# Where a two-way expert stage is joined: the joined norm moved into both ways, and identity products on TensorE around the join

## The reference

```python
def first_block(x, ...):
    for l in range(DEPTH):                                  # DEPTH = 2
        x = x + token_mixers(rmsnorm(x, mix_norm_g[l]), ...)
        h = rmsnorm(x, ffn_norm_g[l])
        if l % 2 == 0:
            x = x + swiglu(h, ffn_w1[l // 2], ffn_w3[l // 2], ffn_w2[l // 2])
        else:
            x = x + moe_ffn(h, router_w[l // 2], moe_w1[l // 2], moe_w3[l // 2], moe_w2[l // 2])
    return rmsnorm(x, final_norm_g)

def second_block(x, c, positions, ...):
    for l in range(DEPTH):
        mod = silu(c) @ ada_w[l] + ada_b[l]                 # shift_m, scale_m, gate_m, shift_f, ...
        h = rms_norm(x, g_pre_mix[l]) * (1.0 + scale_m) + shift_m
        q, k, v, u = split(h @ w_in[l] + b_in[l])
        ...
```

## Time and profile before

| | us |
|---|---|
| median of three runs | 2087.17 |
| lowest and highest of them | 2086.82, 2090.17 |
| the profiled execution | 2089.91 |
| its span, first to last instruction | 2088.1 |
| PE busy in it | 2020.0 |
| mean granted clock of TensorE | 0.988 |

### The profile page before, as it was taken

One profiled execution on the slowest core, in us unless ns is written; L12 is line 12 of the kernel. 1 busy time (PEld: TensorE's weight loads), 2 busy tenths in 40 slices (PEclk: granted clock), 3 DMA queues, 4 the chain that ended last, 5 costly groups with the idle time before them and its releaser, 6 DMA issues.

```text
span 2088.1 us, 24564 instructions
## 1 busy us (share of the span) xinstructions
PE 2020.0 (97%) x10120; PEld 1675.5 (80%) x10120; DVE 1627.6 (78%) x1556; ACT 1187.9 (57%) x1264; POOL 72.8 (3%) x97
## 2 busy tenths in 40 slices
PE   7999999999999999999999999999979999899998
PEld 6888788878887778888888888888767787787887
DVE  5777889756878779888988888888976986676454
ACT  6444454446454367777777777777735444444443
POOL 0000010000000000000000000001010000100000
PEclk9999999999999989999999999999989999999999
DMA  8443479854444458999999999999953898434551
GB/s 307 156 162 139 144 282 386 333 212 179 162 143 155 150 229 331 378 367 379 360 376 370 355 378 377 386 374 385 397 206 132 339 372 302 184 137 173 190 182 61
DMA packets 80321, 554.77 MB, mean 266 GB/s; under 512 B 9286, under 2 KB 11206, under 8 KB 14534
## 3 DMA queue, kind: packets, MB, share of 16 engines
q1 hardware_dynamic: 74160, 536.45, 67.9%
q10 hardware_dynamic: 5468, 14.60, 1.9%
q0 software_dynamic: 576, 2.10, 0.3%
HBM read 548.30 MB, written 4.82 MB: 265 GB/s over the span
## 4 chain that ended last, share of the span: by engine, by line
PE 86%; DVE 8%; ACT 3%; POOL 1%; issue 1%; DMA 1%; ACTq 0%; POOLq 0%; DVEq 0%
PE bank L455 81%; PE bank L482 2%; DVE wlo L1135 2%; ACT whi L1128 1%; POOL small L2363 1%; DVE xn L1715 1%; DMA raw<-in_moe_up 1%; DVE scoresB L1727 1%; DVE gate_tanh L1711 0%; DMA cols<-in_cols 0%; DVE x L2112 0%; DVE xn L2122 0%; PE bank L575 0%; PE bank L960 0%; DVE hTlo L1639 0%
## 5 line engine op out<-in xcount | busy, mean ns | idle before, releaser
L1135 DVE TENSOR_TENSOR wlo<-raw,whi 128x2048 fp32r<-128x2048 f32 x459 | 1045.5, 2285 | 268.1 <-ACT whi L1128 265.2
L1128 ACT ACTIVATE whi<-raw 128x2048 fp32r<-128x2048 f32 x459 | 876.2, 1913 | 355.5 <-PE bank L455 286.5
L455 PE MATMUL bank<-whi,hThi 128*128 128x512 f32 (+1 forms) x1088 | 430.0, 395 | 17.0 <-DVE hTlo L1639 7.4
L455 PE MATMUL bank<-whi,hTlo 128*128 128x512 f32 (+1 forms) x1088 | 421.7, 388 | 0.0
L455 PE MATMUL bank<-wlo,hThi 128*128 128x512 f32 (+1 forms) x1088 | 421.7, 388 | 0.0
L455 PE MATMUL bank<-whi,slots_hi 128*128 128x512 f32 x704 | 275.1, 391 | 2.4 <-DVE wlo L1135 2.3
L455 PE MATMUL bank<-whi,slots_lo 128*128 128x512 f32 x704 | 274.3, 390 | 0.0
L455 PE MATMUL bank<-wlo,slots_hi 128*128 128x512 f32 x704 | 274.2, 389 | 0.0
L455 PEld LDWEIGHTS bank<-whi,hThi 128*128 128x128 f32 x1088 | 208.0, 191 | 69.6 <-issue 14.0
L455 PEld LDWEIGHTS bank<-whi,hTlo 128*128 128x128 f32 x1088 | 208.1, 191 | 41.7
L455 PEld LDWEIGHTS bank<-wlo,hThi 128*128 128x128 f32 x1088 | 208.2, 191 | 39.5 <-issue 1.0
(11 more groups left out here) (332 smaller groups left out, 2269.8 us busy)
## 6 DMA issues: line engine op xcount, KB each, us to landing
raw<-in_moe_up SPq DMA_DIRECT2D x176, 1024.0 KB, 7.1
raw<-in_moe_down SPq DMA_DIRECT2D x88, 1024.0 KB, 7.0
raw<-in_w_in SPq DMA_DIRECT2D x72, 1024.0 KB, 4.8
raw<-in_ada_w SPq DMA_DIRECT2D x48, 1024.0 KB, 6.9
raw<-in_second_up SPq DMA_DIRECT2D x44, 1024.0 KB, 4.9
raw<-in_ffn_up SPq DMA_DIRECT2D x22, 1024.0 KB, 5.3
raw<-in_second_down SPq DMA_DIRECT2D x22, 1024.0 KB, 5.0
raw<-in_w_out SPq DMA_DIRECT2D x16, 1024.0 KB, 5.2
```

The lines of the kernel that those rows point to most:

```text
L455: m = mm(dst, l_, r_, start=start and i == 0, stop=stop and i == len(pairs) - 1)
L1128: s.then_inc(s.unit.activation(split_slots(p)[0][:, 0:n], slot_of_ring(raw, p, NRAW)[:, 0:n], ACT.Copy), ("hi", p), sem="weights_hi")
L1135: e.then_inc(e.unit.tensor_tensor(lo[:, 0:n], slot_of_ring(raw, p, NRAW)[:, 0:n], hi[:, 0:n].bitcast(F32), ALU.subtract), ("lo", p), sem=sem)
```

## The change

The joined norm of ACT and DVE is emitted inside each way, behind the engine's `_way_end` and behind the waits of `ways_joined`, which move there too; the jump over the other way comes after it. PE's waits stay behind its jump. In the joined norm both engines now split piece `q2` 0 ahead, before the features of tile 1. `normed(0)` stays behind the jump. PE gets `keep_clock`: 13 products of the identity with itself at the end of the sparse way, before PE raises its `_way_end`, and six behind the join; they write 128 columns of bank 7, which nobody reads. The dense way gets the six alone.

```diff
+            def keep_clock(n):
+                t.wait_ge(("free", t.held[7]) if 7 in t.held else None)
+                for i in range(n):
+                    m = mm(banks[7][:, 0:P], ident, ident, start=True, stop=True)
+                t.then_inc(m)
...
                 for step in behind_chunks:
                     run(step)
+                keep_clock(13)
...
                     two_ways(t, lambda: sparse_experts(l), lambda: dense_experts(l))
+                    keep_clock(6)
                     t.ahead = AHEAD
...
-        def two_ways(e, sparse, dense):
+        def two_ways(e, sparse, dense, behind=None):
...
                 e.own()
                 board.part = ""
                 e.unit.sem_inc(board.sem(e.done + "_way_end"), 1)
+                if behind is not None:
+                    e.passed, e.last = dict(start["passed"]), None
+                    ways_joined(e)
+                    behind()
                 return e.pieces, [e.counts.get(z) for z in ("weights_hi", "weights_lo")]
...
-            e.passed, e.last = dict(start["passed"]), None
+            if behind is None:
+                e.passed, e.last = dict(start["passed"]), None
+                ways_joined(e)
             if isinstance(e, Tensor):
                 e.held = {}
-            ways_joined(e)
...
+            def joined():
+                square_sum(x3[:, 1], 1, 1, ("squares", "final", 1))
+                features((0, "mix2"), None, (0,))
+                s.wait_ge(("gained", 1))
+                s.own()
+                square_sum(xn3[:, 1], 1, 3, ("squares", "modulated", 0, 0, 1))
+                load_attention(0)
+                s.split_ahead(("q2", 0, 0), 1)
+                features((0, "mix2"), None, (1,))
...
-                    two_ways(s, lambda: sparse_experts(l), lambda: dense_experts(l))
-            square_sum(x3[:, 1], 1, 1, ("squares", "final", 1))
-            features((0, "mix2"), None, (0,))
-            s.wait_ge(("gained", 1))
-            s.own()
-            square_sum(xn3[:, 1], 1, 3, ("squares", "modulated", 0, 0, 1))
-            load_attention(0)
-            features((0, "mix2"), None, (1,))
+                    two_ways(s, lambda: sparse_experts(l), lambda: dense_experts(l), joined)
             load_gate(0, 0)
...
                     v.then_inc(tensor(scaled[:, tt], xn3[:, tt], m3[:, 1, :], ALU.mult))
                     shift(tt)
+                v.split_ahead(("q2", 0, 0), 1)
                 features((0, "mix2"), None, (1,))
-                normed(0)
...
-                    two_ways(v, lambda: sparse_experts(l), lambda: dense_experts(l))
-            joined()
+                    two_ways(v, lambda: sparse_experts(l), lambda: dense_experts(l), joined)
+            normed(0)
```

## The result

The changed kernel takes 2090.81 us (median of 19 runs, 2087.54 to 2099.05) against 2086.24 for the kernel before (19 runs beside them): a ratio of 1.0023, 95% interval 1.0015 to 1.0031. That is 4.6 us slower. The forecast was 1.1 us slower (2088.2 against 2087.17); the time lies inside the range, 0.4 us from its upper end (2091.2), and the forecast has the right sign but a quarter of the size.

The account below looks back on a forecast made before the run. PE was taken as the bound, busy 2020.0 of 2088.1 us, losing most at the join. The terms moved the turn of the keys from 1547.23 to 1548.3, +1.1 us on 2087.17: 2088.2, range 2084.5 to 2091.2.

Parts of the forecast that it names:

- PE, the products: Around PE's jump at the join: thirteen products take 3.1 us, six take 2.6; the first turn comes 1.3 late.
- The clock: In PE's jump at the join, 3.95 us of standing: the clock falls, so the six products run at 1.2 GHz.
- From the first turn to the second: On PE behind the join: the turns of tile 1 come at 1538.0, 0.8 us behind the 1537.23 of before.
- DVE's piece split ahead: On DVE behind tile 1's shift: the 2.25 us piece is hidden just so by PE's work.
- The jumps themselves: Behind tile 1's features: ACT's jump 2.6 us, DVE's 2.9; ACT is the later, 1545.2 against 1544.75.
- 1.83 for `normed(0)`, bias and copies: On DVE behind its 2.9 us jump: this work takes 1.83 us, so DVE is through at 1544.75.
- The second fall of the clock: While PE stands 2.1 us ahead of the keys: a fall adds up to 2.4 us, in the range, not the sum.
- Rival (2): ACT's and DVE's moved jumps cost up to 2.6 us more under DMA load: +3.7, +6.1 with second fall; chance 0.17.
- Rival (1): The clock holds through PE's jump at the join, keys turn at 1545.95: -1.3 us, 2085.9; chance 0.17.
- Rival (3): PE's jump is short and the products work; tile 0's shift is the bound: about -3.8 us, 2083.4; chance 0.06.
- The measure: PE's turn of the keys, 1547.23 before: order and work behind it stay the same, so its shift is the end's.

Follow-up runs that it names:

- e3: The kernel before with the identity products alone (thirteen at the end of the sparse way, six behind PE's jump): ratio 1.0000 to the kernel before.
- e1: The changed kernel with eight one-column memsets ahead of DVE's first wait: ratio 1.0012 to the kernel before.
- e6: The same code as e1, run again: ratio 1.0013 to the kernel before.
- e9: The changed kernel with 128 one-column memsets ahead of DVE's first wait: ratio 1.0047 to the kernel before.
- e5: The kernel before with thirty one-column memsets ahead of DVE's first wait, so a border lies five instructions behind its landing: ratio 1.0018 to the kernel before.
- e4: The changed kernel with ACT's three loads moved from behind its jump into the first attention: ratio 1.0011 to the kernel before.
- e2: The changed kernel without the identity products, both the thirteen and the six: ratio 1.0028 to the kernel before.
- e11: e8 with one line changed, the attention's loads issued at the start of ACT's joined norm instead of right ahead of its jump: ratio 0.9997 to the kernel before.
- e12: e11 with the six identity products put back behind the join: 2085.53 us against 2089.52, ratio 0.9987 to the kernel before.
- e7: The changed kernel without identity products, with eight memsets ahead of DVE's first wait and ACT's three loads in the first attention: ratio 1.0020 to the kernel before.
- e8: The changed kernel with tile 1's features behind the jump, no products, no split ahead, sixteen memsets ahead of DVE's first wait: ratio 1.0006 to the kernel before.
- e10: e7 with no piece split ahead and sixteen memsets instead of eight: ratio 1.0004 to the kernel before.

## Why the prediction was right in sign and short in size

**PE, the products: right.** 3.06 us for thirteen (3.1 said), 3.69 in the jump (3.95), 2.90 for the six (2.6). The first turn came 0.85 us later by its distance; 1.3 was said. **The clock: right**, it fell in PE's jump. **From the first turn to the second: right in kind.** The second turns stand 0.28 us later than in before, 0.8 was said; e3 points to where the rest went, a clock that returns sooner behind the products, but between e1 and e6 this column differs by 0.95. **DVE's piece split ahead: right**, hidden: the low parts of tile 1 start at 1535.91, where 1535.82 was to be had.

**The jumps themselves: right in the sum, wrong in which is the later.** DVE 3.3 (2.9 said), ACT 2.4 (2.6 said). ACT was put last, but its high part of q2 1 was ready by 1543, before DVE wanted it at 1545.63. Without the 4.37 us the keys would have come 26.94 us behind the last scatter product, 0.28 later than in before (26.66); 1.1 was said, and e1, in which nothing but DVE's place in its code differs, measured 26.53.

**The step that failed is the term "1.83 for `normed(0)`, bias and copies" behind DVE's jump.** From the start of `normed(0)` to the weight piece it measured 6.32 us (1539.31 to 1545.63), of which 4.37 were standing still; the work, 1.95, was as said. The sum let DVE run freely once its jump was over. It had asked only what the jump itself costs, and not whether the code behind the landing is there. Shown by e1, e9 and e5: the stall is tied to a place in DVE's code, five instructions behind the landing, that eight more instructions move away and 128 bring back; shown by e4 and e5: it is 1.8 with less under way and 1.2 with an idle DMA, where the full one makes 4.4. That DVE waits there for its next block of code is argued from this and from the packet that ends 1.4 us before DVE goes on (1.39 in after, 1.43 in e2 and e9); no row names the wait.

**The second fall of the clock** was kept out of the sum and put at up to 2.4. It came, and cost 14.57 less 12.11, 2.46 us. Whether it comes in each execution isn't shown: the medians lie 4.6 apart, the stretch of the profiled execution 7.1.

**How far the whole times bear this out.** They show the loss of 4.6 us, and e11 and e12 that it goes when the products are out of the way's end and the jumps stand in a wait with a quiet DMA. They don't show it for the border alone: e1 and e6 lie at 1.0012 and 1.0013, some 2.6 us above before, though their stretch is as short as its, and e9 and e5 lie 5.7 and 3.8 us higher than their stretch says. Where those microseconds go stays open.

**Luck.** That the time lies inside the range owes something to chance. The range reached up to 2091.2 for dearer jumps and not for this stall, and it was set on a median of three runs, 2087.17; with that median the same ratio would have given 2092.0, outside. By the prediction's own terms (1.6 and 2.6 on 2087.17) the upper end is 2091.4 and not 2091.2, and 2084.5 follows from neither the whole spread of the runs nor half of it.

**Rival (2) was the right mechanism in the wrong place.** It said that code comes by the same engines as the transfers, 2.6 us dearer for a jump at a DMA share of 0.96, in all +3.7, or +6.1 with the second fall. In the stretch it was +4.65 at the keys and +7.1, and the sign that was to make it this rival, an issue gap of over 4 us on ACT or DVE, came with the 4.37 us, only not in the jump. The price per jump is confirmed by e2 and e7 (5.3 to 5.4 on DVE instead of 2.8 to 3.3) and e8 (5.3 on ACT instead of 2.4 to 2.6), but in the changed kernel DVE's branch and w_out's transfer came together (1536.0 and 1536.03) and the jump paid only some 0.4 us; what followed its landing paid. A chance of 0.17 for this rival, and 0.11 for slower by more than 0.2% (the ratio is 1.0023), looks too little: the one row with a small transfer in a full queue, 5.2 us to land, spoke for it, and no row against it. That transfer was issued at 1532.95, right behind 1.4 MB of other loads, and not at 1540 to 1543; so it stands for an order of issue, the one of e2, e7 and e8. The Trainium skill, Runtime: NRT & Kernel Launch, Instruction fetch mechanics, was cited for it and held for the jumps, 2.4 to 5.4 us each on ACT and DVE with a packet of code behind the branch. The same section says that the next block is fetched while the present one runs and that crossing a border is mostly hidden; here it was not hidden, 1.17 us with an idle DMA and 4.37 with a full one, and the blocks on this queue were of 8 KB where it names 16 KiB.

**Rival (1)** fell with the clock. **Rival (3)** fell with PE's branch, 3254 ns; that the products return something to the clock is borne out by e3 and e12, but in e3 it is worth about what they cost on the path.

**The measure**, the turn of the keys, wasn't enough: behind it the clock differed, as the range had allowed for.

## What to carry to other kernels

A jump over a large block of code can be followed by a second price, as here: the block behind the landing. Where a branch goes, ask what has been issued to the DMA just ahead of it, by any engine, and how many instructions lie between the landing and the next border of a block; move the transfers ahead or behind (e11), or the code by a few idle instructions (e1), before moving work across the branch. Work moved ahead of this join paid only when the jumps then fell into a wait and an almost empty queue: 2.3 us of 2087 in the stretch of one profile (e11), against 4.6 lost in the medians without that care.

## What the runs showed of the hardware that was not expected

- Right behind a jump, at a place in DVE's code that fits a border between two 8 KB blocks, the engine stands for 1.17 us at a DMA share of 0.03 and for 3.54 to 4.37 at about 1.0, in the middle of instructions that wait for nothing; the profile names it "issue".
- DVE's jump costs 2.8 to 3.3 us or 5.3 to 5.4, by whether a transfer of 1 MB was issued with or behind it, or 0.2 us and more ahead of it.
- PE's branch took 5372 ns in e10 against 3254 to 3952 in the others whose branch is named here; it was hidden. The next 16 KB packet of the other instruction queue (q8) started 2.95 us behind that branch, in the others 0.8 to 1.4; why isn't shown.
- A one-column memset on DVE takes 0.03 us (eight in 0.26), so moving code by a few places is nearly free where the engine waits anyway.
